# Eight experts of a two-layer decoder step: 96 rows each, weights as whole rows, the down product one expert late, no engine loops

## The reference

```python
def moe(x, w_router, wg, wu, wd):
    logits = x @ w_router
    vals, idx = lax.top_k(logits, TOP_K)                 # TOP_K = 2 of N_EXPERTS = 8
    wts = jax.nn.softmax(vals, axis=-1)
    gates = sum(one_hot(idx, N_EXPERTS) * wts[..., None], axis=-2)
    for e in range(N_EXPERTS):                           # D_FF_EXPERT = 1408
        y = y + gates[..., e:e+1] * swiglu(x, wg[e], wu[e], wd[e])
```

## Time and profile before

| | |
|---|---|
| median of 3 timed runs | 1023.94 us |
| span of the profiled execution | 1022.8 us |
| what lies around the span (median less span) | 1.1 us |
| TensorE matmul busy | 967.5 us (95%) |
| TensorE weight load busy | 875.3 us (86%) |
| VectorE busy | 722.5 us (71%) |
| ScalarE busy | 514.5 us (50%) |
| GpSimd busy | 138.4 us (14%) |
| DMA | 224.58 MB, mean 220 GB/s |
| the chain that ended last | TensorE 83%, VectorE 6%, ScalarE 5% |

### The profile page before, as it was taken

One profiled execution on the slowest core, in us unless ns is written; L12 is line 12 of the kernel. 1 busy time (PEld: TensorE's weight loads), 2 busy tenths in 40 slices (PEclk: granted clock), 3 DMA queues, 4 the chain that ended last, 5 costly groups with the idle time before them and its releaser, 6 DMA issues.

```text
span 1022.8 us, 15663 instructions
## 1 busy us (share of the span) xinstructions
PE 967.5 (95%) x6183; PEld 875.3 (86%) x6183; DVE 722.5 (71%) x804; ACT 514.5 (50%) x506; POOL 138.4 (14%) x172
## 2 busy tenths in 40 slices
PE   4999999999999989999899999999999999999974
PEld 4999899999999989988678788787878797888864
DVE  4785576555655778755458896988788896989853
ACT  5321455343444553224346765767476755666542
POOL 4226121101100353341000000000000000000013
PEclk9999899999999999989679999999999999999977
DMA  9934155486358466433058996999789996999801
GB/s 324 321 123 124 41 177 166 140 247 203 120 153 269 148 199 197 143 98 92 33 180 293 363 318 209 334 342 318 278 283 329 347 313 208 339 338 340 289 2 43
DMA packets 153020, 224.58 MB, mean 220 GB/s; under 512 B 5378, under 2 KB 105858, under 8 KB 152816
## 3 DMA queue, kind: packets, MB, share of 16 engines
q1 hardware_dynamic: 150944, 216.64, 63.4%
q0 software_dynamic: 2016, 7.09, 2.2%
HBM read 220.18 MB, written 3.99 MB: 219 GB/s over the span
## 4 chain that ended last, share of the span: by engine, by line
PE 83%; DVE 6%; ACT 5%; DMA 2%; issue 2%; POOL 2%; SPq 0%; DVEq 0%; ACTq 0%; POOLq 0%
PE bank L673 12%; PE bank L674 12%; PE bank L675 12%; PE bank L898 8%; PE bank L899 7%; PE bank L900 7%; PE bank L916 3%; PE bank L917 3%; PE bank L918 3%; ACT whi L1060 3%; DVE wlo L1268 3%; PE bank L876 3%; PE bank L877 1%; PE bank L931 1%; POOL ssum L1716 1%
## 5 line engine op out<-in xcount | busy, mean ns | idle before, releaser
L1268 DVE TENSOR_TENSOR wlo<-raw,whi 128x2048 fp32r<-128x2048 f32 (+3 forms) x222 | 471.9, 2141 | 108.6 <-ACT whi L1060 108.3
L1060 ACT ACTIVATE whi<-raw 128x2048 fp32r<-128x2048 f32 (+3 forms) x222 | 383.9, 1761 | 103.6 <-PE bank L675 64.1
L673 PE MATMUL bank<-xh,whi 128*128 128x264 f32 x672 | 195.9, 292 | 13.8 <-DVE xl L1280 13.8
L674 PE MATMUL bank<-xl,whi 128*128 128x264 f32 x672 | 193.0, 287 | 0.0
L675 PE MATMUL bank<-xh,wlo 128*128 128x264 f32 x672 | 192.8, 287 | 0.0
L898 PE MATMUL bank<-whi,xeh 128*128 128x512 f32 (+1 forms) x384 | 148.6, 387 | 7.0 <-DVE wlo L1268 5.4
L900 PE MATMUL bank<-whi,xel 128*128 128x512 f32 (+1 forms) x384 | 144.7, 377 | 0.0
L899 PE MATMUL bank<-wlo,xeh 128*128 128x512 f32 (+1 forms) x384 | 144.7, 377 | 0.0
L673 PEld LDWEIGHTS bank<-xh,whi 128*128 128x128 f32 x672 | 129.4, 193 | 15.4 <-DVE wlo L1268 10.7
L674 PEld LDWEIGHTS bank<-xl,whi 128*128 128x128 f32 x672 | 129.4, 192 | 0.2
L675 PEld LDWEIGHTS bank<-xh,wlo 128*128 128x128 f32 x672 | 128.6, 191 | 0.0
(11 more groups left out here) (224 smaller groups left out, 1426.0 us busy)
## 6 DMA issues: line engine op xcount, KB each, us to landing
raw<-in_moe_w_down SPq DMA_DIRECT2D x40, 1024.0 KB, 5.3
raw<-in_moe_w_gate SPq DMA_DIRECT2D x32, 1024.0 KB, 5.6
raw<-in_moe_w_up SPq DMA_DIRECT2D x32, 1024.0 KB, 6.3
raw<-in_w_in SPq DMA_DIRECT2D x20, 1024.0 KB, 9.2
raw<-in_moe_w_gate SPq DMA_DIRECT2D x16, 768.0 KB, 4.6
raw<-in_moe_w_up SPq DMA_DIRECT2D x16, 768.0 KB, 4.6
raw<-in_ffn_w_down SPq DMA_DIRECT2D x16, 704.0 KB, 4.7
raw<-in_ffn_w_gate SPq DMA_DIRECT2D x10, 1024.0 KB, 6.1
```

Source lines behind the costliest of these rows:

```text
L673: pe.matmul(out, w_hi, x_hi, start=start, stop=False)
L674: pe.matmul(out, w_hi, x_lo, start=False, stop=False)
L1060: act.activation(whi[off % SPL][:, 0:n], raw[off % RAW][:, 0:n], ACT.Copy).then_inc(hi_ready, 1)
L1268: dve.tensor_tensor(wlo[off % SPL][:, 0:n], raw[off % RAW][:, 0:n], whi[off % SPL][:, 0:n].bitcast(F32), ALU.subtract).then_inc(lo_ready, 1)
```

## The change

- The list of an expert has 96 places (`CAP`), so that the stationary operands of the experts' products have 96 columns, the one-hot matrix of a pair has 192, and hidden values and results have 96 rows. Above 96 tokens the general path is taken.
- The weights come as whole rows: a gate or up unit is 128 rows of 1408 columns, 16 units per expert (gate and up by turns), and six units of down weights of 2 x 1024 columns (the last 1 x 1024), 22 units per expert in place of 18. Each gate/up unit serves all three steps (512, 512, 384), with six banks open.
- The order is `PHASES`: gate/up of 0, gate/up of 1, down of 0, gate/up of 2, down of 1, and so on. silu and `hid` of an expert are made once, behind its gate/up; its transposes stand in the down product of the expert before, its scatter in the gate/up of the second expert after it.
- ScalarE and VectorE work three units ahead in the experts.
- The third block of 8 tokens is padded with zeros to 128 rows (two memsets on GpSimd), and all gather matmuls have 128 rows. Of the first pair only two of four gather steps stand ahead of the first unit, the others behind units 1 and 3. A later pair is gathered in the down product of an even expert.
- Norm factor, gate values and token number of each place come from one small fp32r product (`slot_values`, 20 columns, 6 matmuls) per pair, which replaces `gather_rstd` and the gate products; the transposed one-hot matrix is made on VectorE by a comparison with a row of token numbers (`trow`, one more DMA on GpSimd's queue).
- `pos` is computed with fp32r operands (6 instructions in place of 12).
- No loops: all turns are written out.

```diff
-CAP = 128
+CAP = 96
...
+GU_UNITS = 2 * DC
+DOWN = ((0, 2), (2, 2), (4, 2), (6, 2), (8, 2), (10, 1))
+PHASES = [("gu", 0)]
+for _e in range(1, NE):
+    PHASES += [("gu", _e), ("d", _e - 1)]
+PHASES.append(("d", NE - 1))
...
+GATHER_AFTER = {0: 0, 2: 1, 3: 2, 4: 3}
+HID_AFTER = {1: (2, 0), 3: (1,)}
+FIRST_GATHER_AFTER = {1: 2, 3: 3}
+FIRST_RG_AFTER = 9
+FIRST_HID_AFTER = {2: 0, 3: 1, 4: 2}
+SCATTER_AFTER = 1
...
+                                load(v % RAW, v - (RAW - 1), src[k * P:(k + 1) * P, :], 1, FE)
...
-                    for j, w in BLK:
-                        out, sel = b[:, 2 * c * P:2 * (c + 1) * P], pick[0:w, j, :, :].rearrange("p a n -> p (a n)")
-                        pe.matmul(out, xth[0:w, j, f:f + P], sel, start=(j == 0), stop=False)
-                        mm = pe.matmul(out, xtl[0:w, j, f:f + P], sel, start=False, stop=(j == 2))
+                    k = 2 * i + c
+                    out = b[:, 2 * c * CAP:2 * (c + 1) * CAP]
+                    for j in range(3):
+                        rows = pick[:, j, :, :].rearrange("p a n -> p (a n)")
+                        pe.matmul(out, xth[:, j, k * P:(k + 1) * P], rows, start=(j == 0), stop=False)
+                        mm = pe.matmul(out, xtl[:, j, k * P:(k + 1) * P], rows, start=False, stop=(j == 2))
...
+            def gate_up(e, i):
...
+                for s, (lo, n) in enumerate(STEPS):
+                    if k == 0 and e == 1:
+                        pe.wait_ge(hid_ready if up else sgate_ready, s + 1)
...
+                    b = bank[3 * up + s][0:CAP, 0:n]
+                    pe.matmul(b, X, H[:, lo:lo + n], start=(k == 0), stop=False)
+                    pe.matmul(b, X, L[:, lo:lo + n], start=False, stop=False)
+                    mm = pe.matmul(b, Y, H[:, lo:lo + n], start=False, stop=(k == DC - 1))
...
+                            down(e, i)
+                            if e < NE - 1 and i in HID_AFTER:
+                                for s in HID_AFTER[i]:
+                                    hid_rows(e + 1, s, bank[s])
+                            if e % 2 == 0 and e + 2 < NE and i in GATHER_AFTER:
+                                p, g = e // 2 + 1, GATHER_AFTER[i]
+                                if g == 0:
+                                    pe.wait_ge(pick_ready, p + 1)
+                                if g < 3:
+                                    pe.wait_ge(hid_ready, 3 * (e + 1) + g + 1)
...
+                                gather(p, g, bank[3 + g % 3])
...
+            def silu_gate(e):
+
+                act.wait_ge(rg_ready, e // 2 + 1)
+                act.wait_ge(unit_used, U_FF[1] + MOE_AT["gu", e] + GU_UNITS - 1)
+                for s, (lo, n) in enumerate(STEPS):
+                    act.activation(hid[0:CAP, lo:lo + n], bank[s][0:CAP, 0:n], ACT.Silu,
+                                   scale=rgs[0:CAP, e // 2 % 2, e % 2, 0:1]).then_inc(sgate_ready, 1)
...
+                        split_next(MOE_AT[kind, e] + i + SPL - 1)
...
+                            if i == GU_UNITS - 1:
+                                hidden(e)
...
+                    pool.memset(xth[:, 2, :].bitcast(F32), 0.0).then_inc(moe_zeroed, 1)
+                    pool.memset(xtl[:, 2, :].bitcast(F32), 0.0).then_inc(moe_zeroed, 1)
...
+                    pool.dma_start(trow[:, :], t["trow"]).then_inc(trow_in, 16)
```

More of the change, by code:

```diff
@@ L536, in side_bank @@
         def side_bank(l, name):
-            return 4 + (0 if name == "over" else SIDE[l, name] % 4)
+            return 7 if name == "over" else 4 + SIDE[l, name] % 4
         def chunk_full(eng, n):
@@ L640, in _ @@
             dense(1, U_WO[1], W_O)
-            experts(Turn("first"))
-            with sp.Fori(0, (NE - 2) // 2) as pair:
-                for half in range(2):
-                    experts(Turn("loop", pair, half))
-            experts(Turn("last"))
-            experts(Turn("tail"))
+            experts()
             dense(1, U_PLE[1], PLEU[:AHEAD])
@@ new lines, in slot_values, with hid_rows @@
+            def slot_values(p, b):
+                pe.wait_ge(rgv_ready, 1)
+                for a in range(2):
+                    for j in range(3):
+                        mm = pe.matmul(b[0:CAP, 2 * VALS * a:2 * VALS * (a + 1)], pick[:, j, a, :],
+                                       rgv[:, j, :, :].rearrange("p h v -> p (h v)"), start=(j == 0), stop=(j == 2))
+                mm.then_inc(rg_full, 1)
+            def hid_rows(e, s, b):
+                pe.wait_ge(hid_ready, 3 * e + s + 1)
+                for c in range(STEPS[s][1] // P):
+                    f = 4 * s + c
+                    mm = pe.transpose(b[:, c * CAP:(c + 1) * CAP], hid[0:CAP, f * P:(f + 1) * P], ident[0:CAP, 0:CAP])
+                mm.then_inc(tr_full, 1)
@@ new lines, in down @@
+            def down(e, i):
+                u = U_FF[1] + MOE_AT["d", e] + i
+                f0, n = DOWN[i]
+                pe.wait_ge(lo_ready, u + 1)
+                H = whi[u % SPL][:, 0:n * D].rearrange("p (k w) -> p k w", k=n)
+                L = wlo[u % SPL][:, 0:n * D].rearrange("p (k w) -> p k w", k=n)
+                if i == 0 and e == 0:
+                    pe.wait_ge(hl_ready, 3)
+                elif i == 0 and e < NE - 1:
+                    pe.wait_ge(h_added, DC * e)
+                elif i == 0:
+                    pe.wait_ge(hid_ready, 3 * NE)
+                for c in range(n):
+                    f = f0 + c
+                    if f % 4 == 0:
+                        pe.wait_ge(hl_ready, hid_turn(e, f // 4) + 1)
+                    X, Y = hh[:, hid_slot(e, f), :], hl[:, hid_slot(e, f), :]
+                    for half in range(2):
+                        b = bank[y_bank(e) + half][0:CAP, :]
+                        own = slice(half * 512, (half + 1) * 512)
+                        pe.matmul(b, X, H[:, c, own], start=(f == 0), stop=False)
+                        pe.matmul(b, X, L[:, c, own], start=False, stop=False)
+                        mm = pe.matmul(b, Y, H[:, c, own], start=False, stop=(f == EC - 1))
+                mm.then_inc(unit_used, 1)
@@ L1022, in _ @@
                 else:
[L1024 to L1036 removed]
+                    experts()
                     pe.wait_ge(hid_ready, 3 * NE)
[L1038 removed]
+                    pe.wait_ge(h_added, DC * NE)
                     with pe.If(pe.value_load(flag[0:1, 0:1], min_val=0, max_val=2 * T) > 0):
@@ L1649, in _ @@
                     route()
-                    for a in range(2):
-                        dve.wait_ge(tmp_full, a + 1)
-                        dve.tensor_copy(rslot[:, a:a + 1], bank[6 + a][:, 0:1]).then_inc(tmp_free, 1)
-                    for i in range(GATHERS):
-                        dve.wait_ge(tmp_full, i + 3)
-                        gathered(i, bank[6 + i % 2], i + 1)
-                    ahead(U_WO[1] + 3)
-                    gates()
-                    run_turn(Turn("first"))
-                    with dve.Fori(0, (NE - 2) // 2) as pair:
-                        for half in range(2):
-                            run_turn(Turn("loop", pair, half))
-                    run_turn(Turn("last"))
-                    run_turn(Turn("tail"))
+                    experts()
                     with dve.If(dve.value_load(flag[0:1, 0:1], min_val=0, max_val=2 * T) > 0):
```

669 lines of the change are left out of this document (307 added, 362 removed).

## The result

The change made the kernel slower: 1036.5 us, median of four runs (1032.9 to 1039.7), against 1023.7 for before; the ratio is 1.012 (95% interval 1.0098 to 1.0142). I had forecast 999. The profiled execution is the quickest of the four, 1032.9; the 3.6 us that the median has above it are in no trace.

A forecast was written before the change was run, and what follows sets the result against it. TensorE was taken to set the experts' time. Terms -12.4 - 1.4 - 13.2 - 10.5 + 2.7 - 5.4 + 13.2 + 3 = -24.0 from 1023.9 gave 999.9, forecast 999 us; 8-in-10 range 980 to 1046.

The forecast's parts named there:

- The ring of raw slots: Landing, copy and split of expert weights: 8.0 us per slot cycle, 2.0 per unit against TensorE's 1.91; 6 us, halved to +3.
- Rival 2: Expert weight slots are the bound: landing 5.6 us, 2.2 us per unit, 24 us in all, 1020 us; chance 0.13.
- The waits that come: TensorE waiting at ends of gate/up phases, mostly for `hid`: 6.6 + 3.6 + 3.0 = +13.2 us, bounds 5 and 25.
- The order argument: At the end of gate/up, `hid` queues behind VectorE's split of the third down unit (2.29 us), ready at 5.0 us.
- The gather: Gather matmuls of 192 columns: 0.111 us each at full clock, 0.160 at 1.2 GHz; later gathers -13.2 us.
- rival 1: Narrow fp32r gather matmuls run at the float32 rate, 0.33 us each: +49 us, 1048 us; chance 0.17.
- Start of the stage: From first one-hot product to first expert: 19.52 us removed, 4.1 and 3.0 put in, net -12.4; `pos` another -1.4.
- transposed one-hot: Transposed one-hot and gates leave TensorE, 1.31 us per expert: -10.5 us; `slot_values` put in: +2.7.
- waits that go: TensorE's waits for `wlo` before units of 2048 columns vanish as engines work three units ahead: -5.4 us.
- Weights: Expert matmuls with 96 stationary columns instead of 128: same 162 + 48 matmuls, counted 0, at best 7 us of gain.
- rival 3: 96 rows count as a change of height, 0.22 us per passage, 176 passages: 39 us, 1038 us; chance 0.05.
- Two experts: Time of a pair in the expert stage: about 105 us where it was 113.6; wrong if over 110.

## Why the prediction was wrong

The times of its own steps against the trace after. With the start of the stage at 499.2, the forecast had the stage 441.7 us long (464.3 - 12.4 - 13.2 - 10.5 + 2.7 - 5.4 + 16.2, of which 16.2 is the 13.2 of new waits and the 3 of the ring) and a tail of 57.9. The profile has 477.2 from 497.8, and 56.1. The stage's 35.5 us too many come from three places, by its window and that of the run with half the bytes: 42.2 us without a matmul where I had 16.2 (+26.0); a busy time of 435.0 against 414.6 for the same instructions (+20.4), most of it the half clock (mean granted 0.96 against 0.99; in windows of 1 us TensorE is busy at the half clock for 36.9 us against 6.6, and half of the difference, an estimate of what it costs, is 15); and less work than I had counted, 414.6 against 425.5 (-10.9). They add up to 35.5.

- **The ring of raw slots** (+3 us) is the step that failed: the waits for `wlo` that it stood for took 19.8 + 1.7 = 21.5 us. Rival 2 (chance 0.13) was the right one in kind, but not in its sign: gate/up units still go at 1.90 (689.89 to 691.79) and not at 2.2, and the loss stands before the first down units, when the reserve is used up. The slot's cycle was worked out rightly, but with the landing of 4.7 us that another stage shows, and its cost halved for longer pieces. Landing is 5.5 to 5.8, and 7.6 for down units: it is no fixed time but grows with what is in flight (the same 704 KB: 4.6 us in the dense feed-forward part of this trace, where the mean DMA share is 0.59 from 240 to 330 us, 5.5 to 5.8 here, 6.0 to 6.1 with a fifth slot). In a cycle of four units (4 x 1.91 = 7.6 us), copy 1.38, split 1.62 and 0.3 leave 4.3 for it; in five units 6.3, and it then measured 6.0 to 6.1. By these figures four lack more than 1 us per round and five have it just covered: the waits for `wlo` went from 23.8 us (with `hid` moved; 17.8 with eight down units) to none. I had also priced all units alike: a down unit of 1.05 MB is asked for at the pace of a gate/up unit, 549 GB/s against the 383 to 408 of full DMA engines, and a gate/up unit itself needs 377.
- **What the change did to the ring** is shorten the cycle; the rate asked for within gate/up is the same. Before, a unit of 1024 KB kept TensorE for 12 x 0.230 = 2.76 us, which is 380 GB/s, no less than now. But four such units last 11.0 us, and landing 5.3 to 6.3, copy 1.91, split 2.29 and 0.3 take 9.8 to 10.8. The new units are a third shorter, and their landing is not. I had not compared the two. Other work stood between the weights all along, too, with a mean of 304; the change put it on one side of the passage. The control with half the bytes, which gained next to nothing, agrees with both; no run parts them.
- The Trainium skill (DMA: Bandwidth & Descriptors, Where 436 GB/s comes from) lets the HBM side bind at some 358 GB/s per core, beside a measured 425 for a transfer of 16 MB. The trace differs: windows at share 1 move 383 to 408 here; the measurement decides. An estimate by the page's figure, 2.01 us to fetch a gate/up unit, is more than TensorE's 1.91 and would have been a warning, though from a figure that this trace does not bear out.
- **The waits that come** (+13.2, bounds 5 to 25): the three gather waits and the one between experts 0 and 1 were there, in their places, and too small: 10.7 where I had 6.6, 4.0 where I had 3.6 for transposes, 3.9 where I had 3.0. 18.6 in all, inside the bounds. In the wait between experts 0 and 1 stands a table load of ScalarE of 1.28 us (538.60), ahead of its first silu, which no row had priced. The order argument was right, and it names the cure: 22.7 us for one call moved.
- **The clock** was no term at all, and no reason was given for leaving it out: the second step that failed. In the passage shown the granted clock is 1.00 through the wait of 2.15 us and falls to 0.50 within that of 4.61; it is back some 4.5 us after TensorE starts again. Over the stage the busy time grew by the 20.4 us above, nearly as much as the `wlo` waits themselves (21.5). The Trainium skill (TensorE: Matmul & The Clock Gate, HAM oscillation — how this bites in real kernels) warns that waits for DMAs between short bursts of matmuls bring the lower clock; the trace agrees, with 4.61 us idle and matmuls 0.43 apart behind it, though this wait ended with `hid` and not with a DMA.
- **The gather** at 0.111: right at full clock, and rival 1 is out. At half clock they double, 703.96 to 706.09 is ten in 2.13, 0.213 each, where I took 0.160 from the columns. So the first 24 took 5.2 us and not 3.8. The first steps of the kernel after, and the same behind unit 1:

```profile
497.84 0.50 PE L798 MATMUL bank<-pick,xth 128*128 128x192 f32 x1 [1.59 <-DVE pick L1499]
498.14 0.42 PE L799 MATMUL bank<-pick,xtl 128*128 128x192 f32 x1
498.36 0.42 PE L798 MATMUL bank<-pick,xth 128*128 128x192 f32 x1
...
507.14 0.27 PE L799 MATMUL bank<-pick,xtl 128*128 128x192 f32 x1
507.25 0.28 PE L798 MATMUL bank<-pick,xth 128*128 128x192 f32 x1
507.37 0.27 PE L799 MATMUL bank<-pick,xtl 128*128 128x192 f32 x1
```

- **Start of the stage, transposed one-hot, waits that go**: in kind right. The first gate/up matmul stands 5.2 us behind the first gather (I said about 4) at a clock of 0.97, where before the first 5 us of the first expert went at 0.50: 2.5 us of the 10.9 that I had not counted. The 8.5 us without a matmul before were 3.1 more than the 5.4 that I took away. The other 5 us I have not taken apart.
- **Weights** at 0.230 and 0.176 (nothing from 96 columns) and no change of height for 96 rows (rival 3): right; scatter matmuls stand 0.12 apart (609.66, 609.78, the next gate/up matmul at 609.90). In the Trainium skill (TensorEngine Tiling (Array Packing)) the modes that rival 3 goes by stand in the section Available Configurations.
- **Two experts** took 118.6 to 120.3 us from silu to silu. I had written that over 110 makes me wrong, and it does. With half the bytes it was 102.4 to 103.1, with the ring of five 103.3 to 103.8: the 105 that I forecast for the change are there once the ring carries it.

What is open: how the 41 us split between the rate of the down units and of gate/up (the halves overlap), how much of the ring of five is the raw slots and how much the unit more of lead, and why the small down unit first was worse. That the medians of some kernels lie up to 9 us above the profiled execution (1031.5 against 1022.5 with eight down units) isn't explained either.

## What to carry to other kernels

Where units of different size share a ring that counts units, work out the bytes asked for per us over each stretch, at the pace of the engine that frees the slots, and compare that with the DMA engines at share 1, not with their mean; then give the ring the landing time under that load, not the one of a quieter stage. Units that get shorter with the same number of slots shorten the cycle in which a load must land, and in this kernel work taken away from between the weights went the same way. A long wait of TensorE costs more than its length: behind the 4.61 us here some 4.5 us of matmuls ran at the half clock, behind 2.15 none did. Look last at what stands in front of the result that others wait for: a product of 2 us behind a split that isn't due for 5 us cost 22.7.

## What the runs showed of the hardware

- Gather matmuls with 128 stationary and 192 moving columns in fp32r stand 0.11 to 0.12 us apart at 2.4 GHz (507.14, 507.25, 507.37) and 0.213 at 1.2 GHz: so what bounds them beside their columns (192 columns alone are 0.080 and 0.160) takes twice as long at half the clock, too.
- Landing of the same 704 KB is 5.5 to 5.8 us with four slots and 6.0 to 6.1 with five, while TensorE no longer waits for it.
- TensorE's granted clock held at 1.00 through a wait of 2.15 us and behind it, and fell to 0.50 during one of 4.61. Through one of 3.56 us (up to 642.38) it held, and fell to 0.50 about 1 us behind it, for some 3 us.
